# Fourier transform over the latent tokens, split into even and odd tokens

## What is computed

```python
def fourier_mix(u):
    B, L, _ = u.shape
    ug = u.astype(F32).reshape(B, L, FNET_GROUPS, FNET_W // FNET_GROUPS)
    y = jnp.fft.fftn(ug, axes=(1, 3), norm='ortho').real
    return y.reshape(B, L, FNET_W).astype(u.dtype)
```

## Time and profile before

| | |
|---|---|
| median of 3 runs | 1126.73 us (1122.79 to 1127.68) |
| the profiled execution | 1123.43 us |
| its span, first to last instruction | 1121.5 us |
| mean granted TensorE clock | 0.959 |
| TensorE matmul / weight load busy | 1007.0 us (90%) / 567.2 us |
| VectorE, ScalarE, GpSimd busy | 388.4, 225.3, 166.2 us |
| "dft" load | 1 DMA, 2048 KB |
| line 800, records of 512 columns | 32, mean 611 ns |
| line 788, records of 256 columns | 20, mean 383 ns |

### The profile page before, as it was taken

The page is one execution under the profiler, slowest core; times in us unless marked ns, Lnnn a source line. Parts: engine busy times, 40 slices in busy tenths (PEclk is TensorE's granted clock), DMA queues, the critical chain, the costliest instruction groups (busy, mean ns, idle before and its releaser), DMA issues.

```text
span 1121.5 us, 10795 instructions
## 1 busy us (share of the span) xinstructions
PE 1007.0 (90%) x4164; PEld 567.2 (51%) x4164; DVE 388.4 (35%) x845; ACT 225.3 (20%) x444; POOL 166.2 (15%) x160
## 2 busy tenths in 40 slices
PE   3899998999799989999999999989957897978875
PEld 1555544655455557777777777745533332322221
DVE  3314331135653523323233233317672232221222
ACT  3213630114254421101011011002111220211111
POOL 0000000010430013122132132100010111111111
PEclk9999999999889999999999999999978998998988
DMA  9634344100000152212213113092169999999993
GB/s 375 284 132 181 150 150 185 69 5 2 1 1 1 57 214 100 98 48 79 72 47 104 47 47 103 13 363 94 59 243 388 359 383 400 403 423 402 404 411 98
DMA packets 36163, 196.12 MB, mean 175 GB/s; under 512 B 7504, under 2 KB 11280, under 8 KB 25872
## 3 DMA queue, kind: packets, MB, share of 16 engines
q1 hardware_dynamic: 31200, 184.40, 41.9%
q0 software_dynamic: 4768, 10.50, 3.9%
q10 hardware_dynamic: 144, 0.52, 0.1%
HBM read 188.13 MB, written 14.09 MB: 180 GB/s over the span
## 4 chain that ended last, share of the span: by engine, by line
PE 82%; DMA 9%; issue 4%; DVE 3%; ACT 1%; POOL 0%; SPq 0%; POOLq 0%; DVEq 0%; ACTq 0%
PE psum L962 22%; PE psum L1143 9%; PE psum L697 8%; PE psum L979 8%; PE psum L1015 6%; PE psum L1159 4%; DMA r_bv<-in_w_e 4%; PE psum L813 3%; PE psum L899 3%; PE psum L698 2%; PE psum L706 2%; PE psum L913 2%; DMA r_w<-h_scratch,tab 2%; DMA r_w<-in_w_ada 2%; PE psum L923 2%
## 5 line engine op out<-in xcount | busy, mean ns | idle before, releaser
L962 PE MATMUL psum<-r_h,r_w 128*128 128x320 f32 x512 | 143.3, 433 | 1.7 <-DVE r_d L1824 1.7
L2248 POOL TENSOR_TENSOR r_w<-r_w 128x512 f32<-128x512 f32 x64 | 80.6, 1270 | 313.1 <-PE psum L962 237.2
L962 PEld LDWEIGHTS psum<-r_h,r_w 128*128 128x128 f32 x512 | 97.2, 190 | 42.3 <-DVE r_d L1824 2.0
L962 PE MATMUL psum<-r_ys,r_w 128*128 128x320 f32 x384 | 108.6, 432 | 0.0
L697 PE MATMUL psum<-r_h,r_w 128*128 128x512 f32 x192 | 98.9, 597 | 1.5 <-DVE r_h L1587 1.5
L962 PEld LDWEIGHTS psum<-r_ys,r_w 128*128 128x128 f32 x384 | 73.0, 190 | 30.4
L1414 ACT ACTIVATE r_bv<-r_bv 128x320 f32<-128x320 f32 x64 | 30.1, 470 | 273.2 <-DVE r_bv L1871 273.2
L1015 PE MATMUL psum<-r_w,r_bv 128*128 128x512 f32 x160 | 74.0, 609 | 3.4 <-DVE r_bv L1866 3.4
L698 PEld LDWEIGHTS psum<-r_h,r_w 128*128 128x128 f32 x192 | 36.5, 190 | 45.9 <-issue 45.9
L2259 POOL DMA_INDIRECT out_y<-r_bv,tab x17 | 26.8, 1576 | 211.7 <-DVE r_bv L2099 191.7
L979 PE MATMUL psum<-r_ys,r_w 128*128 128x320 f32 x192 | 55.6, 432 | 0.0
(11 more groups left out here) (378 smaller groups left out, 1624.4 us busy)
## 6 DMA issues: line engine op xcount, KB each, us to landing
r_a<-in_w_ada SPq DMA_DIRECT2D x8, 2048.0 KB, 7.9
r_w<-in_w_gate SPq DMA_DIRECT2D x32, 512.0 KB, 4.6
r_a<-in_w_e SPq DMA_DIRECT2D x6, 2048.0 KB, 32.3
r_c<-in_w_e SPq DMA_DIRECT2D x6, 2048.0 KB, 32.8
r_w<-in_w_e SPq DMA_DIRECT2D x5, 2048.0 KB, 35.9
r_ys<-in_w_e SPq DMA_DIRECT2D x4, 2048.0 KB, 35.4
r_bv<-in_w_e SPq DMA_DIRECT2D x4, 2048.0 KB, 37.5
r_h<-in_w_e SPq DMA_DIRECT2D x4, 2048.0 KB, 36.2
```

What stands on the lines that cost most here:

```text
L962: ins = mm(gate_bank(u, n), w[:, k, :], x[:, k, :], start=(k == 0), stop=(k == HK - 1))
L2248: g.tensor_tensor(w_mix[n], x, y, op).then_inc(s_wm, 1)
```

## The change

The latent tokens are regrouped into even and odd ones. With N = 512 the transform over the tokens at frequency k + 256 is that of the even tokens at k minus that of the odd tokens at k, and at k it is their sum. So only frequencies 0 to 255 are multiplied:

- "fa": the stationary operand of a latent tile is every second token (256 of them in two tiles) instead of 128 in a row; the order of the tiles is even 0, even 1, odd 0, odd 1.
- "fy": 8 products of 256 columns; the even tiles add up in columns 0 to 255 of the bank, the odd ones in 256 to 511.
- VectorE takes the context columns with a copy, copies the odd part to `yf`, then writes sum and difference.
- SyncE loads from the same matrix in DRAM only frequencies 0 to 255, rows in the order of the new tiles: 8 DMAs with pieces of 1 KB, each to 64 partitions, 1 MB in all; the semaphore counts follow.

```diff
--- before.py
+++ after.py
@@ -127,6 +127,15 @@
 RING_USES[0].append("woutA")
 RING_USES[1].append("woutB")
 USE = {n: (slot, i) for slot, names in enumerate(RING_USES) for i, n in enumerate(names)}
+RING_LOADS = {"dft": 8}
+
+
+def ring_count(name):
+
+    slot, i = USE[name]
+    return 16 * sum(RING_LOADS.get(n, 1) for n in RING_USES[slot][:i + 1])
+
+
 LAST_JOB = {"win0": "c1", "win1": "gl1", "win2": "uf1", "dft": "fy1", "qkvA": "qkv4", "qkvB": "qkv4", "wq": "q4"}
 
 UNITS = [(2 * p + j, t) for p in range(H // 2) for t in range(TT) for j in range(2)]
@@ -499,7 +508,7 @@
         def ring_wait(eng, name):
 
             slot, i = USE[name]
-            eng.wait_ge(ring_loaded[slot], 16 * (i + 1))
+            eng.wait_ge(ring_loaded[slot], ring_count(name))
             return wring[slot]
 
         def gate_bank(u, n):
@@ -559,7 +568,14 @@
             ring("ada6", a["w_ada"][6])
             ring("win2", a["w_in"][2])
             ring("ada7", a["w_ada"][7])
-            ring("dft", a["dft"])
+            ring_free("dft")
+            dft = a["dft"].rearrange("(m q) (g h s n) -> q g h m s n", q=2, g=2, h=2, s=2)
+            for q in range(2):
+                for g in range(2):
+                    for h in range(2):
+                        at = (q * 2 + g) * NLAT
+                        sp.dma_start(wring[0][h * 64:(h + 1) * 64, at:at + NLAT].rearrange("p (s n) -> p s n", s=2),
+                                     dft[q, g, h, :, :, 0:NLAT // 2]).then_inc(ring_loaded[0], 16)
             for i in range(8, ADA_CHUNKS):
                 ring(f"ada{i}", a["w_ada"][i])
             ring("qkvA", a["w_qkv"][0])
@@ -785,20 +801,22 @@
             for t in range(TT):
                 o = begin(f"fa{t}")
                 for j in range(2):
-                    ins = mm(o[:, j * 256:(j + 1) * 256], uf[:, j, t * P:(t + 1) * P], const("cs64"),
-                             start=True, stop=True)
+                    x = uf[:, j, t * P:(t + 1) * P] if t == LT else \
+                        uf[:, j, 0:NLAT].rearrange("p (g m q) -> p q g m", g=2, q=2)[:, t // 2, t % 2]
+                    ins = mm(o[:, j * 256:(j + 1) * 256], x, const("cs64"), start=True, stop=True)
                 ins.then_inc(filled, 1)
 
             modulation(11)
             wait_drained(pe, *[f"fa{t}" for t in range(TT)])
-            w = ring_wait(pe, "dft").rearrange("p (t s n) -> p t s n", t=LT, s=2)
+            w = ring_wait(pe, "dft")[:, 0:LT * NLAT].rearrange("p (t s n) -> p t s n", t=LT, s=2)
             wc = const("dftc").rearrange("p (s n) -> p s n", s=2)
             for j in range(2):
                 o = begin(f"fy{j}")
                 for t in range(LT):
+                    q, g = divmod(t, 2)
                     for s in range(2):
-                        mm(o[:, 0:NLAT], af[:, t, j * 256 + s * P:j * 256 + (s + 1) * P], w[:, t, s, :],
-                           start=(t == 0 and s == 0), stop=(t == LT - 1 and s == 1))
+                        mm(o[:, q * 256:(q + 1) * 256], af[:, t, j * 256 + s * P:j * 256 + (s + 1) * P], w[:, t, s, :],
+                           start=(g == 0 and s == 0), stop=(g == 1 and s == 1))
                 for s in range(2):
                     ins = mm(o[:, NLAT:NT], af[:, LT, j * 256 + s * P:j * 256 + (s + 1) * P], wc[:, s, :],
                              start=(s == 0), stop=(s == 1))
@@ -1693,7 +1711,11 @@
                 v.tensor_copy(af[:, t, :], o[:, 0:512]).then_inc(drain(f"fa{t}"), 1)
             for j in range(2):
                 o = take(dve, f"fy{j}")
-                v.tensor_copy(yf[:, j, :], o[:, 0:NT]).then_inc(drain(f"fy{j}"), 1)
+                even, odd = yf[:, j, 0:NLAT // 2], yf[:, j, NLAT // 2:NLAT]
+                v.tensor_copy(yf[:, j, NLAT:NT], o[:, NLAT:NT])
+                step(v.tensor_copy(odd, o[:, NLAT // 2:NLAT]))
+                step(v.tensor_tensor(even, o[:, 0:NLAT // 2], odd, ALU.add))
+                v.tensor_tensor(odd, o[:, 0:NLAT // 2], odd, ALU.subtract).then_inc(drain(f"fy{j}"), 1)
 
             def latents(t):
```

## The result

| | before | after |
|---|---|---|
| median | 1126.73 us (1122.79 to 1128.22, 7 runs) | 1118.36 us (1115.85 to 1119.75, 7 runs) |
| ratio | 1 | 0.9938 (95% interval 0.9922 to 0.9955) |
| the profiled execution / its span | 1123.43 / 1121.5 us | 1115.85 / 1113.9 us |
| mean granted TensorE clock | 0.959 | 0.961 |

The change is faster by 0.6%. The forecast was 1119.9 us with a range of 1115.5 to 1124.5, and "faster by over 0.5%" had 0.63. The lines of the kernel moved: 706 is now 722, 788 is 806, 800 is 818, 803 is 821, 813 is 831, 843 is 861, 1696 became 1715 to 1718.

The account below looks back on a forecast made before the run. TensorE was taken as the bound, busy 90% of the span and 82% of the chain. Halved Fourier products save 6.8 us, all else nothing: 1126.73 - 6.8 = 1119.9 us, range 1115.5 to 1124.5.

Parts of the forecast that it names:

- The products: Fourier products on TensorE: 256-column records at 0.216 us in place of 0.429, saving 6.8 us over both halves.
- The first group: First Fourier group, 0.69 us longer than the second: claimed to be low clock ending at its own time, so it stays.
- A2: Rival: no clock fall at the first stall before the Fourier products, 1.9 us less, 1118.0 us; chance 0.06.
- The strided operand: Columns products (fa), weights read with a step of two: taken as zero, at most 2.6 us, covered by a DMA wait.
- VectorE: VectorE's pieces after each Fourier half: 2.0 us, 1.2 more than before, bounds 1.3 and 3.6; cost nothing.
- The cover I named: VectorE's idle time behind the two Fourier halves, 6.49 and 9.45 us before, claimed to hide its added work.
- The load: Eight matrix DMAs on SyncE's queue: 2.6 to 5.6 us of issue, chunk 8 off 2.4 to 5.3 later; cost nothing.
- Rival D: The eight loads land one after the other, so modulation chunk 8's product waits: 1145.6 us; chance 0.03.
- the argument with chunk 8: Modulation chunk 8's load, delayed behind the eight, still precedes its product at 142.18; DMA traffic had ended by 135.
- What comes next: Stages from q/kv and keys on: no load or other engine tied to its own time, so 6.8 us reach the end.
- The clock: Rival: TensorE's half-clock stretches after stalls vary; one more or longer 1124.9 us (0.13), no first fall 1118.0 (0.06).

Follow-up runs that it names:

- regrouped, 512 frequencies: After with all 512 frequencies, the full 2 MB in eight loads, 512-column products and the old single copy: 1127.03 us, ratio 1.0002 to before.
- one load: After with the half matrix laid out beforehand in the new order, one DMA of 1 MB in place of eight: 1118.51 us, ratio 0.9921 to before.
- VectorE three times: After with VectorE's copy, sum and difference of each half done three times: 1117.84 us, ratio 0.9917 to before.
- VectorE eight times: After with VectorE's copy, sum and difference of each half done eight times: 1121.87 us, ratio 0.9967 to before.
- 32 loads: After with each of the eight matrix loads cut into four of 16 partitions: 1125.22 us, ratio 0.998 to before.
- before with the products four times: Before with the eight latent Fourier products carried out four times for each channel half, 96 more records of 512 columns: 1167.24 us, ratio 1.0363.
- the second of after: The profile of after, unchanged, from a second set of runs: that set measured 1120.59 us, ratio 0.995 to before.
- after with the products four times: After with its eight latent Fourier products carried out four times for each channel half, 96 more records of 256 columns: 1141.72 us, ratio 1.0115 to before.

## Why the prediction was right, step by step

**The products: right in mechanism and size.** The step "a record of 256 columns costs 0.216 us, from the spacing of line 788" held to the hundredth: 3.46 us for the second group, and 0.216 again with 64 records in a row. The sum of 6.8 us came out as 6.8 from fa to q/kv. At full clock a first group takes 7.06 with 512 columns and 3.65 with 256, a second one 6.87 and 3.46, so the products alone give 3.41 + 3.41 = 6.82. The balance above is these 6.82, plus 0.17 because the low clock cost 1.49 in place of 1.66 (the table below), less 0.20 for the longer wait. That these two cancel, so that 6.8 came out to the tenth, is luck.

**The first group: the sum was right, the split of it wrong.** I wrote that the 0.69 us by which the first group exceeds the second is low clock and stays. It is 0.19 of transition, which stays, and 0.50 of clock. The clock's part wanders between the modulation product and the group behind it, so the two are taken together. At full clock they take 1.92 + 7.06 = 8.98 us with 512 columns and 1.92 + 3.65 = 5.57 with 256. In the executions with a fall they took longer by:

| | modulation product | first group | above full clock |
|---|---|---|---|
| before | 3.08 | 7.56 | 1.66 |
| regrouped, 512 frequencies | 3.42 | 7.06 | 1.50 |
| after | 3.41 | 3.65 | 1.49 |
| one load | 3.32 | 3.91 | 1.66 |
| VectorE three times | 2.46 | 4.75 | 1.64 |
| VectorE eight times | 3.17 | 4.05 | 1.65 |
| 32 loads | 3.26 | 3.65 | 1.34 |

The eighth profile with a fall, before with the products four times, fits: 3.43 + 27.66 against 1.92 + 7.06 + 3 x 6.87 is 1.50. A fall costs 1.3 to 1.7 us, whatever the width of the products and wherever it lies. A2 had it at 1.9, since it counted the 0.19 too and took 1.85 for a modulation product that takes 1.92 in this place. So the half of my sentence that counts, the stretch ends at its own time and not after a number of products, held: the change neither shortened nor lengthened it. Where it would lie was not to be had from one trace.

**The strided operand: nothing, and not only because of the cover.** I had taken zero, with 2.6 us as the end from above. The copies of "fa" stay 0.865 us apart, and 20 records take 4.54 against 4.53 us when nothing hides them. The doubled weight load is excluded: it takes 0.194 us against 0.189. By the rule of the Trainium skill (SBUF — State Buffer, section "Door 1: The DMA port swizzle"), reads are at full rate as long as two of them fall into one line, and this trace agrees.

**VectorE: over-priced, without effect.** 1.54 us for a half in place of 2.0, between the bounds of 1.3 and 3.6. The narrow copy took 0.29 and not 0.42, and the engine's wait on its own semaphore some 0.04 (186.03 + 0.41 to 186.48) and not 0.17: that row was the wait behind an instruction of 640 columns, and why it is longer isn't shown. The cover I named was right, and the eightfold version shows that it ends.

**The load: within the bounds, close to the upper one.** 5.42 us of issue (2.6 to 5.6 had been given), chunk 8 off 6.1 us later than before (128.72 against 122.58). Of these, 2.6 are the later start that this execution brought along (123.26 against 120.69), and 3.6 come from the eight issues. I had overlooked that in before the queue paused between the issue of the matrix, over at 121.02, and that of chunk 8 at 122.58: the buffer that chunk 8 goes into comes free only then. That pause takes up 1.6 us of the added issues, so the delay to expect was 0.7 to 3.7 us and not 2.4 to 5.3. The error was on the safe side. No wait followed, as said. That the eight issues are hidden is shown by the one load, which gives the same time; that 32 loads bring the wait shows that the argument with chunk 8 was the one to make. Rival D, loads that land one after the other, is out: 2.8 us each from the issue (3.1 at most), all eight by 131.2. As for the port rule of the Trainium skill (SBUF — State Buffer, the same section), which spoke against this load with 196 GB/s for 64 partitions: with an issue every 0.68 us for 128 KB, the queue offered on average only some 193 GB/s, so these runs don't show whether the ports would have given more.

**What comes next: right.** The first key product came at 240.57, not 238.0, and q/kv at 189.52, not 186.9. Both are later by the 2.6 us that after had lost before 61 us. The distance between them (50.9 us) and the stage up to the merge's end (330.9) are as before, and no other later stage of the table is longer by more than 0.1. Nothing took the gain back.

**The clock: the rival was there, and under-rated.** A2 had "no fall at the first stall" at 0.06. It happened in two of ten profiles with this wait (the second of after, and after with the products four times), the others being the seven of the table and before with the products four times. The two had the shortest waits, 3.30 us each, against 3.35 to 3.61 in the eight with a fall. So the length of the wait may be what decides, or the moment at which it falls; the runs don't tell these apart. My condition for A2, that the strided loads make the wait shorter, is not it, as after had both 3.30 and 3.58. The Trainium skill (TensorE: Matmul & The Clock Gate, section "What's actually happening") has the moment hang on a counter that runs freely, so that equal kernels differ; two executions of after did. Whether a gain by A2 reaches the end can't be told from one pair of profiles, of which the one without the fall was the longer. The mean granted clock goes with much of what is left. Over 166 executions of all these kernels, with a level of its own for each kernel, the time is 0.55 us longer for each 0.001 of mean clock less, and what remains scatters with a standard deviation of 1.7 us.

**The size.** All executions set against their clock, at 0.957: before 1126.4, after 1118.7 us, 7.7 less with a standard error of 0.5. The difference of the medians in the first set, 8.4 us, is larger than that, the second set's, 5.0, smaller. Whether the 0.9 over the forecast's 6.8 is real isn't settled: no stage of the profiles holds it, and the profile's clock has the gap named above. The two profiled executions differ by 7.6 us, of which 6.8 lie in the stage of the change; the other stages differ by up to 2.6 us either way.

## What to carry to other kernels

Where one engine makes over 80% of the chain, price a change by the spacing of records of the new shape from elsewhere in the same trace, not by their mean durations; here that gave the 6.82 us of the products at full clock. Then name, for each thing that the change adds to another engine or queue, the next instruction that waits behind it and by how much it is early: 8.1 us for chunk 8 and 8.7 for VectorE were the two numbers that decided it. And look for work that can be moved into a stall next to the edit: the wait for the last modulation chunk was worth 4 to 5 us more, over half of the change itself, once each product waited for its own tile alone.

## What the runs showed of the hardware that was not expected

- Float32 weights read from SBUF with a step of two elements cost nothing: 4.54 against 4.53 us for 20 records.
- In one kernel, a wait of 3.30 us for a load was followed by a product of 1.92 us at a granted clock of 1.00, one of 3.58 by one of 3.41 at 0.56; a fall of the clock costs 1.3 to 1.7 us there, before it has come back.
- The profile's clock can read 1.00 near the start while records run at half their pace: 3.69 us for 16 records in after at 22 us, where later chunks take 1.85 to 1.90.
- Issuing one DMA took SyncE 0.33 us for the 2 MB matrix in one, 0.68 on average for 64 partitions with two pieces of 1 KB each, and for 16 such partitions 0.49 on average (median 0.42).
- The kernel before, 1.12 ms long, scatters with a standard deviation of 2.4 us over 69 executions, much of it with the mean granted clock.
